# Later token groups of a mixture-of-experts layer: 32 rows over four column groups of the array instead of 64 rows over two

## The reference

```
N_GROUPS, EXP_PER_GROUP, N_EXPERTS, TOP_K, D_EXPERT = 4, 8, 32, 2, 256

def hier_moe(h, w_group, w_router, w_gate, w_up, w_down):
    g_logits = h @ w_group;  g_idx = argmax(g_logits);  g_p = max(softmax(g_logits))
    e_logits = the 8 logits of group g_idx from w_router
    top_p, top_i = top_k(softmax(e_logits), 2);  top_p = top_p / sum(top_p)
    combine[t, e] = g_p * top_p for the two chosen experts, else 0
    gate, up = h @ w_gate[e], h @ w_up[e]            # 1024 -> 256 each
    act = silu(gate) * up * combine
    return sum over e of act @ w_down[e]             # 256 -> 1024
x = x + hier_moe(rms_norm(x));  y = rms_norm(x)
```

## Time and profile before

| | |
|---|---|
| median of 3 runs | 758.47 us |
| lowest and highest | 752.69 and 758.62 us |
| the profiled execution | 756.18 us, span 754.4 us |
| granted TensorE clock, mean over the span | 0.940 of 2.4 GHz |
| busy share of the span | PE 85%, PEld 62%, DVE 48%, ACT 27%, POOL 17% |

### The profile page before, as it was taken

One profiled execution on the slowest core, in us unless ns is written; L12 is line 12 of the kernel. 1 busy time (PEld: TensorE's weight loads), 2 busy tenths in 40 slices (PEclk: granted clock), 3 DMA queues, 4 the chain that ended last, 5 costly groups with the idle time before them and its releaser, 6 DMA issues.

```text
span 754.4 us, 12453 instructions
## 1 busy us (share of the span) xinstructions
PE 644.7 (85%) x4508; PEld 467.1 (62%) x4509; DVE 362.0 (48%) x681; ACT 200.9 (27%) x403; POOL 130.6 (17%) x229
## 2 busy tenths in 40 slices
PE   5999999999699989989999839787777999799830
PEld 5999988899689889864455635344433554444410
DVE  4658778699685576546655541121121111112138
ACT  6553566313133241250111201111111111111113
POOL 0000102022400010030011163212213123222110
PEclk9999999999799999996999959999999999999985
DMA  9322322322550000025911154999999999959835
GB/s 283 88 72 77 105 79 63 85 57 41 157 205 2 1 1 1 1 92 198 374 46 43 45 196 148 413 413 413 415 415 410 396 375 352 413 213 391 333 138 219
DMA packets 72922, 146.50 MB, mean 194 GB/s; under 512 B 14136, under 2 KB 50316, under 8 KB 64543
## 3 DMA queue, kind: packets, MB, share of 16 engines
q1 hardware_dynamic: 67039, 137.17, 49.2%
q0 software_dynamic: 5824, 8.54, 3.2%
HBM read 139.44 MB, written 16.60 MB: 207 GB/s over the span
## 4 chain that ended last, share of the span: by engine, by line
PE 67%; DMA 17%; DVE 10%; issue 3%; ACT 2%; SPq 1%; POOLq 0%; POOL 0%; DVEq 0%; ACTq 0%
PE ps L1762 20%; PE ps L2080 16%; DMA wd<-w_down 13%; PE ps L1852 9%; PE ps L2002 7%; DMA xg<-h_rows,gcur 2%; DVE XX L1465 2%; DVE x L1681 1%; PE ps L1786 1%; PE ps L2105 1%; PE ps L1775 1%; PE ps L2024 1%; PE ps L1711 1%; DMA expert_rows<-yo,osid 1%; PE ps L1964 1%
## 5 line engine op out<-in xcount | busy, mean ns | idle before, releaser
L2080 PE MATMUL ps<-gu,xT 128*64 128x256 f32 x1024 | 132.4, 404 | 30.3 <-DMA wd<-w_down 26.4
L2080 PEld LDWEIGHTS ps<-gu,xT 128*64 128x64 f32 x1024 | 73.2, 144 | 85.9 <-issue 35.0
L1762 PE MATMUL ps<-hhi,whi 128*128 128x256 f32 (+1 forms) x416 | 119.5, 287 | 3.1 <-DVE wlo L1176 1.6
L1762 PE MATMUL ps<-hlo,whi 128*128 128x256 f32 (+1 forms) x416 | 117.3, 282 | 0.0
L1762 PE MATMUL ps<-hhi,wlo 128*128 128x256 f32 (+1 forms) x416 | 117.2, 282 | 0.0
L1634 DVE SCALAR_TENSOR_TENSOR gact<-gth,ps 128x128 f32<-128x128 f32 x32 | 9.2, 288 | 161.0 <-ACT gth L940 161.0
L1762 PEld LDWEIGHTS ps<-hhi,whi 128*128 128x128 f32 x416 | 78.3, 188 | 9.1 <-issue 6.2
L1762 PEld LDWEIGHTS ps<-hhi,wlo 128*128 128x128 f32 x416 | 78.4, 189 | 0.0
L1762 PEld LDWEIGHTS ps<-hlo,whi 128*128 128x128 f32 x416 | 78.2, 188 | 0.0
L2080 PE MATMUL ps<-wd,aT 128*64 128x512 f32 x256 | 62.2, 607 | 0.4 <-ACT aT L944 0.4
L2002 PE MATMUL ps<-wout,yT 128*128 128x512 f32 x128 | 57.7, 599 | 0.0
(11 more groups left out here) (372 smaller groups left out, 979.4 us busy)
## 6 DMA issues: line engine op xcount, KB each, us to landing
gu<-w_gate SPq DMA_DIRECT2D x32, 1024.0 KB, 10.2
gu<-w_up SPq DMA_DIRECT2D x32, 1024.0 KB, 12.4
wd<-w_down SPq DMA_DIRECT2D x32, 1024.0 KB, 15.6
wraw<-w_in SPq DMA_DIRECT2D x26, 512.0 KB, 3.8
wout<-w_out SPq DMA_DIRECT2D x1, 4096.0 KB
yk<-expert_rows SPq DMA_DIRECT2D x8, 512.0 KB, 5.8
x<-x_prompt SPq DMA_DIRECT2D x4, 512.0 KB, 6.3
s<-state_delta SPq DMA_DIRECT2D x4, 512.0 KB, 6.1
```

Source lines behind the costliest of these rows:

```text
L1762: last = mm(ps[:, 2 * (n % 2) + half, 0:hi - lo], weights[:, c, :], h[:, c, lo:hi], start=c == 0 and j == 0, stop=c == KT - 1 and j == len ...
L2080: last = mm(ps[g * CAP:(g + 1) * CAP, bank, 0:width], left(c), right(c, g), start=c == 0, stop=c == steps - 1)
```

## The change

Groups after the first hold 32 rows (`OVER`) instead of 64, and there may be up to 15 of them instead of 8. The stationary operand of their matmuls is 32 columns wide, and `quarters` gives each of four column groups of the array a quarter of the weights' columns. A program matmul of `up_more` streams 128 columns instead of 256, one of `down_more` 256 instead of 512, and there are twice as many. The turn of the activations becomes two ordinary matmuls by columns of the identity, since the four quarters have to be regrouped. The tiles between shrink: `xTo`, `oth`, `oact`, `oaT`, `yo` have half the columns, `xo` half the rows. The scatter writes quarter rows (128 rows of 1 KB) instead of half rows (128 rows of 2 KB). The index lists grow from 8 to 15 groups.

```
-MAXROWS = 9 * CAP
-MORE = MAXROWS // CAP - 1
+OVER = 32
+MORE = 15
+MAXROWS = CAP + MORE * OVER
...
-            for half in range(2):
-                sp.dma_start(oraw[half * CAP:(half + 1) * CAP], tab.rearrange("(g r e) o -> r g (e o)", r=CAP, e=NE)[:, 1:]).then_inc(
+            for q in range(4):
+                sp.dma_start(oraw[q * OVER:(q + 1) * OVER], tab[CAP * NE:, :].rearrange("(g r e) o -> r g (e o)", r=OVER, e=NE)).then_inc(
                     slots_in, 16)
...
-                copy(xTo[:, :, :].rearrange("p a b -> p (a b)"), ps[:, 3, :], ACT.Copy).then_inc(m_act, 1)
+                copy(xTo[:, :, :].rearrange("p a b -> p (a b)"), ps[:, 3, 0:KT * OVER], ACT.Copy).then_inc(m_act, 1)
...
-                nc.vector.tensor_copy(yo[:, :], ps[:, 3, :]).then_inc(m_vec, 1)
+                nc.vector.tensor_copy(yo[:, :], ps[:, 3, 0:D // 4]).then_inc(m_vec, 1)
...
+            def quarters(left, right, steps, width):
+                for c in range(steps):
+                    for q in range(4):
+                        last = mm(ps[q * OVER:(q + 1) * OVER, 3, 0:width], left(c), right(c, q), start=c == 0, stop=c == steps - 1)
+                return last
...
             def up_more(u, done):
                 pe.wait_ge(m_act, done * 3 + 1)
-                up(u, 3, lambda c: xTo[:, c, :]).then_inc(m_pe, 1)
+                quarters(lambda c: xTo[:, c, :], lambda c, q: gu[u][:, :, c, q * P // 2:(q + 1) * P // 2], KT, P).then_inc(m_pe, 1)

             def down_more(u, done):
                 pe.wait_ge(m_vec, done * 3 + 3)
-                turn(ps[:, 3, 0:P], oact[:, :], ident).then_inc(m_pe, 1)
+                by_quarter = ident.rearrange("p (a b r) -> p b a r", a=2, b=2)
+                for b in range(2):
+                    last = mm(ps[b * P // 2:(b + 1) * P // 2, 3, 0:P // 2], oact[:, :], by_quarter[:, b], start=True, stop=True)
+                last.then_inc(m_pe, 1)
                 pe.wait_ge(m_act, done * 3 + 3)
-                down(u, 3, oaT).then_inc(m_pe, 1)
+                quarters(lambda c: oaT[:, c * OVER:(c + 1) * OVER], lambda c, q: wd[u][:, c, q * D // 4:(q + 1) * D // 4], 2,
+                         D // 4).then_inc(m_pe, 1)
```

More of the change, by code:

```diff
@@ L47 @@
 CAP = 64
-MAXROWS = 9 * CAP
-MORE = MAXROWS // CAP - 1
+OVER = 32
+MORE = 15
+MAXROWS = CAP + MORE * OVER
+assert MAXROWS >= T
 NOWHERE = 1 << 20
@@ L75 @@
 C_GIR = C_REV + NE
-C_HALF = C_GIR + NE
-C_BEFORE = C_HALF + 1
+C_QUARTER = C_GIR + NE
+C_BEFORE = C_QUARTER + 1
 C_PID = C_BEFORE + 1
@@ L101, in constants @@
     c[:, C_GIR:C_GIR + NE] = 99 - np.arange(NE) // EG
-    c[:, C_HALF] = p // CAP
+    c[:, C_QUARTER] = p // OVER
     c[:, C_BEFORE] = p // CAP - 2
@@ L105, in constants @@
     c[:, C_SLOT:C_SLOT + P] = np.arange(P) % CAP
-    c[:, C_CAPS:C_CAPS + MORE] = CAP * np.arange(1, MORE + 1)
+    c[:, C_CAPS:C_CAPS + MORE] = CAP + OVER * np.arange(MORE)
     for t, tile in enumerate(ORDER):
@@ L309, in build @@
         scur = [moe2(f"scur{s}", [P, 1], I32) for s in range(4)]
-        xTo = moe2("xTo", [P, KT, CAP])
+        xTo = moe2("xTo", [P, KT, OVER])
         moref = moe2("moref", [1, NE, MORE])
         morec = moe2("morec", [1, NE])
-        oth, oact, oaT = (moe2(n, [P, P]) for n in ("oth", "oact", "oaT"))
-        yo = moe2("yo", [P, D // 2])
+        oth, oact, oaT = (moe2(n, [P, P // 2]) for n in ("oth", "oact", "oaT"))
+        yo = moe2("yo", [P, D // 4])
         otok = [moe2(f"otok{u}", [P, 1], I32) for u in range(4)]
@@ L322, in build @@
         osids = further("osids", [P, MORE * NE], I32)
-        xo = [further(f"xo{u}", [CAP, D]) for u in range(4)]
+        xo = [(further if u < 3 else moe)(f"xo{u}", [OVER, D]) for u in range(4)]
         sfin = late("sfin", [P, H, P])
@@ L900, in more_rows_out @@
                 act.wait_ge(m_pe, done * 4 + 1)
-                copy(xTo[:, :, :].rearrange("p a b -> p (a b)"), ps[:, 3, :], ACT.Copy).then_inc(m_act, 1)
+                copy(xTo[:, :, :].rearrange("p a b -> p (a b)"), ps[:, 3, 0:KT * OVER], ACT.Copy).then_inc(m_act, 1)
             def more_tanh(done):
                 act.wait_ge(m_pe, done * 4 + 2)
-                copy(oth[:, :], ps[:, 3, 0:P], ACT.Tanh, scale=0.5).then_inc(m_act, 1)
+                copy(oth[:, :], ps[:, 3, 0:P // 2], ACT.Tanh, scale=0.5).then_inc(m_act, 1)
             def more_act_T(done):
                 act.wait_ge(m_pe, done * 4 + 3)
-                copy(oaT[:, :], ps[:, 3, 0:P], ACT.Copy).then_inc(m_act, 1)
+                copy(oaT[:, :], ps[:, 3, 0:P // 2], ACT.Copy).then_inc(m_act, 1)
             def later(g, done):
@@ L1103, in save_more @@
                         pool.sem_inc(cleared, 1)
-                        nc.gpsimd.indirect_dma_start(out=yd, out_offset=bass.IndirectOffsetOnAxis(ap=osid[:, 0:1], axis=0),
-                                                     in_=yo[:, :], in_offset=None, bounds_check=4 * T - 1,
+                        nc.gpsimd.indirect_dma_start(out=yd.rearrange("r (q d) -> (r q) d", q=2),
+                                                     out_offset=bass.IndirectOffsetOnAxis(ap=osid[:, 0:1], axis=0),
+                                                     in_=yo[:, :], in_offset=None, bounds_check=8 * T - 1,
                                                      oob_is_err=False).then_inc(m_out, 16)
@@ L1137, in _ @@
                 link(nc.gpsimd.memset(t[:, :], 0))
-            pool.wait_ge(slots_in, 3 * 16)
+            pool.wait_ge(slots_in, 5 * 16)
             slot_of, past = (t[:, :, :].rearrange("p a b -> p (a b)") for t in oidf)
@@ L1143, in _ @@
             link(nc.gpsimd.tensor_copy(otoks[:, 0:MORE * NE], past))
[L1144 removed]
+            link(nc.gpsimd.tensor_scalar(osids[:, :], slot_of, 4.0, cst[:, C_QUARTER:C_QUARTER + 1], ALU.mult, ALU.add))
             pool.wait_ge(routed, NT + 1)
@@ L2112, in turn_more @@
                 for c in range(KT):
-                    out, part = ps[:, 3, c * CAP:(c + 1) * CAP], xo[u][:, c * P:(c + 1) * P]
+                    out, part = ps[:, 3, c * OVER:(c + 1) * OVER], xo[u][:, c * P:(c + 1) * P]
                     if c == 0:
-                        mm(out, part, ident[0:CAP, 0:CAP], start=True, stop=True)
+                        mm(out, part, ident[0:OVER, 0:OVER], start=True, stop=True)
                     else:
-                        ins = turn(out, part, ident[0:CAP, 0:CAP])
+                        ins = turn(out, part, ident[0:OVER, 0:OVER])
                 ins.then_inc(m_pe, 1)
```

6 lines of the change are left out of this document (3 added, 3 removed).

## The result

The changed kernel takes 833.2 us (median of 4 runs, 827.9 to 836.5) against 757.1 us before in the same session (4 runs, 752.7 to 758.6): **1.1015 of the time before, 95% interval 1.0977 to 1.1053**. It is 10% slower, where 751.0 us was forecast and 745 to 757 was the range.

The account below looks back on a forecast made before the run. DMA weight loading was taken as the bound, with 11.4 us idle around experts with a second group. Savings on PE and in copies, limited by POOL, summed to 6.3 us: 749.9 profiled, 752.2 as median, 751.0 taken; range 745 to 757.

Parts of the forecast that it names:

- The change part by part: Step costing the matmuls, turns, copies, scatter and work ahead of the loop, each by its expected change in time.
- the slow side: Rival: four column groups take turns instead of streaming together, the end comes 15.8 us later, 772; chance 0.03.
- The sum: Savings followed from expert 17 to the load issued after expert 24's release: 6.3 us gained, decided by POOL's path.
- Up: Up products of a further group on PE: 64 matmuls at 27 ns plus 0.2 for width changes, 1.93 instead of 3.46.
- u: Time saved per expert on a further group's up products: 1.5 us, 1.15 at 33 ns, about 0 at 52 ns.
- The Trainium skill's 62 ns: Pace making up 4.0 us; near the rival of instructions 63 ns apart, 757.9 to 760.2, chance 0.05.
- Down: Down products of a further group on PE: 16 instructions at 52 ns plus 0.1, so 0.95 us instead of 1.77.
- d: Time saved on a further group's down products: 0.8 us.
- Copy of yo: DVE copy of yo, 256 columns for 512: 0.42 us instead of 0.69, 0.27 saved.
- Scatter of yo: Transfer after experts 19 and 23, same 128 indices, half the bytes: kept at 6.94 us, 8.33 the dear end.
- The gather behind expert 19: Gather xg that PE waits for: its landing and PE's restart at 646.00 move by 4.1 us, to near 642.
- The end: Expert 28's load to the finish: 6.3 us earlier, last load landing near 709, everything after it in fixed order.

Follow-up runs that it names:

- experiment 8: The kernel before plus 172 never-run PE instructions per expert, with only a quarter of the weights loaded from the fifth expert on: 794.1 us (one run).
- experiment 1: The changed kernel without PE's code for an expert's third and later groups, which no expert here enters: 749.88 us, 0.993 of before.

## Why the prediction was wrong

**The step that failed** is the list of what the change adds, in *The change part by part*. Up, down, turns, copies, scatter and index lists are costed there by the instructions that an expert with a further group executes. The code that stands in the program and is not executed got neither a term nor a bound: 86 instructions more in each of two copies for each of four experts, 688 in a round. They cost 833.2 - 750.6 = 82.6 us, by the kernel in which the same instructions run in the same order: 833.2 - 767.0 = 66.2 go when the jump is announced and nothing is loaded again, 13.2 for each of five jumps back, and 767.0 - 750.6 = 16.4 stay. None of the rivals held it either; the one on the slow side, four groups taking turns on the array, was the wrong mechanism, and its 772 lay 61 us short. What could have been read: the earlier trace rows show which code runs, and the trace's view of the queues has no packet of code between 550 and 700 us, so a round was visibly staying on the engine; how far it was from not staying was not asked. The trace of before could not have said where the step lies.

**The steps that can be read from the kernels whose code stays.** The sum was a gain of 6.3 us, the forecast 5.3 to 7.3. Without `later` the gain is 755.5 - 749.9 = 5.6 us, written once it is 756.2 - 750.6 = 5.6 us, each against the kernel before beside it. That is inside the forecast, but not every term came out, and the two profiled executions below lie 3.6 and 1.2 us above their kernels' medians.

*Up.* Forecast 1.93 us, u = 1.5; measured 1.88, u = 1.58. The 64 matmuls stand (1.96 - 0.273) / 63 = 26.8 ns apart, so the 27 was right; 1.88 - 64 x 0.0268 = 0.16 is left of the 0.2 that was set aside for changes of width. The Trainium skill's 62 ns for a matmul that the sequencer's code decodes (TensorE: Matmul & The Clock Gate, the section on 56 ns against 53.3 ns), which the prediction weighed as a rival, isn't the pace of this stretch.

*Down.* Forecast 0.95; its 16 matmuls take 1.07 and 0.22 follow before the next product, 1.29, so d is 0.5 and not 0.8 there. In the kernel written once the wait behind expert 17 is 0.90 and uses d up: 604.24 - 602.27 = 1.97, against 1.77 before. In the sum d counts once, for expert 17, so 0.3 and 1.0 us of the 6.3 are missing here.

*Copy of yo.* Forecast 0.42, measured 0.42 (DVE, before 0.69).

*Scatter of yo.* Kept at 6.94. The chain of waits of the kernel without `later`, and then that of the one written once:

```profile
623.28 8.12 DMA expert_rows<-yo,osid
...
635.64 8.66 DMA xg<-h_rows,gcur
...
693.26 18.07 DMA wd<-w_down
```

```profile
623.89 6.65 DMA expert_rows<-yo,osid
...
634.77 7.79 DMA xg<-h_rows,gcur
...
692.39 17.13 DMA wd<-w_down
```

8.12 in one execution and 6.65 in the other for the same transfer: the bound of 8.33 was needed, the prediction's sign that this term failed (later than 7.5) stands in one of two, and single profiles don't settle the term. The 1.5 us are found again further on. The gather behind expert 19 is still what PE waits for, as forecast, near 642: the wait ends at 644.34 and at 642.68, where it was 646.00, so it moved by 1.7 and 3.3 instead of 4.1.

*The end.* Expert 28's load is issued at 675.39 and at 673.86 against 678.89: 3.5 and 5.0 earlier, not 6.3. The last load lands at 693.26 + 18.07 = 711.3 and at 692.39 + 17.13 = 709.5, against 715.5, so 4.2 and 6.0 earlier; 709 was forecast. The spans end 2.7 and 4.4 earlier (751.7 and 750.0 against 754.4), so some 1.5 us of it is lost behind that load, where the prediction took the order as fixed; where, isn't shown. The windows that answer to the earlier trace rows, of the kernel written once:

```profile
596.00:608.00 12.00, 10.78 (x142) 6.24 (x142) 2.14 (x6) 1.28 (x5) 2.23 (x3) 1.00 0.98 390
616.00:628.00 12.00, 10.41 (x135) 6.16 (x137) 2.71 (x8) 1.61 (x6) 3.40 (x5) 1.00 0.98 383
656.00:668.00 12.00, 9.92 (x127) 6.37 (x128) 1.68 (x5) 1.33 (x5) 2.23 (x3) 0.86 0.93 364
668.00:684.00 16.00, 14.77 (x119) 7.83 (x119) 3.23 (x9) 2.81 (x7) 4.54 (x8) 1.00 0.71 269
```

The DMA's share is 0.98 in both earlier gaps, and 12 x 0.07 + 16 x 0.29 = 5.5 us idle from 656 to 684 stay: "gone" and "some 5", as forecast. In the kernel without `later` the same four shares are 0.92, 0.98, 0.80 and 0.67: 1.0 of the first gap stays, and 12 x 0.20 + 16 x 0.33 = 7.7 us from 656 to 684.

*Ahead of the loop.* The longer index lists showed once, as 0.52 us of PE's wait for gathered rows at 471.43 in the kernel without `later`; 0.5 was the dear end.

So the mechanism that was forecast is there and gives 5.6 us, and a second one, which the prediction left out, takes fifteen times as much.

## What to carry to other kernels

A branch that is never taken isn't free: inside a loop its code takes room on the engine, and once the loop's written code no longer stays there, each jump back loads it again (here 9 packets and some 13 us a jump). Before costing what a change executes, count what it writes in the loop for each engine, and look at the packets of the instruction queue and at "issue" waits at the loop's head; a loop that is near its limit is mended by writing a body once under conditions (all of the 83 us here), or in part by announcing the jump back (66 of them, which left the kernel 1.3% above the one before). When a loss shows in stages that the change doesn't touch, look for something that they share with it, as here the room for code.

## What the runs showed of the hardware

- Without an announcement a PE loop of 1531 instructions stayed and one of 1787 was loaded anew at each jump back, in 9 packets of 16 KB; with it 1964 stayed and 2476 didn't. The Trainium skill, Runtime: NRT & Kernel Launch (Instruction fetch mechanics), gives TensorE room for 2048 instructions, refilled in 16 KiB blocks of 256. The packets agree in size, and 2048 lies in the announced bracket; not announced, the limit lies lower. The same section says that a long kernel need not fit and calls the cost of crossing into the next block mostly hidden, but also that a taken branch to code that isn't held stalls until it is fetched; here loading the loop again cost 66.2 us.
- The five jumps back to code that isn't there stop PE for 11.7, 11.7, 11.9, 6.2 and 5.5 us in the changed kernel, beside a DMA at 0.84, 0.89, 0.98, 0.68 and 0.65 of its throughput. With a quarter of the weights (experiment 8) they are 4.7 to 10.0 us beside 0.42 to 0.59, where the same code with all weights has 4.7 to 11.8. Behind a long one some 2.7 us more are lost, since the first products after the idle time run at a granted clock of 0.50 (3.68 us for 16 that take 1.90).
- Code on the first way through is not free either beside a DMA at 0.95 of its throughput (476 to 529 us): 4 x 64 unused instructions in a round cost 16.3 us of issue waits in that stretch (2.6 in the whole loop before), and 9.5 us of the time.
- Fp32 matmuls of 128 columns in four column groups stand 26.8 ns apart, weight loads between them (experiment 1).
